# VectorE's order in the halves of an expert ring: dots, weights and rows first, its piece of attention or normalisation last

## What is computed

```python
def block_tail(x, mix, w_out, ln_g, ln_b, w_pq, sub_keys, u_tab, v_tab):
    h = layer_norm(ALPHA * x + mix @ w_out, ln_g[0], ln_b[0])
    return layer_norm(ALPHA * h + peer_ffn(h, w_pq, sub_keys, u_tab, v_tab), ln_g[1], ln_b[1])

# in peer_ffn, for a block of 128 tokens:
    q = (xb @ w_pq).reshape(PEER_BLOCK, PEER_HEADS, 2, PEER_QDIM // 2)
    s = jnp.einsum('phcd,hckd->phck', q, sub_keys).astype(jnp.float32)
    ts, ti = lax.top_k(s, PEER_TOPK)
    ...
    fs, fpos = lax.top_k(cand.reshape(PEER_BLOCK, PEER_HEADS, -1), PEER_TOPK)
    eidx = jnp.take_along_axis(cidx.reshape(PEER_BLOCK, PEER_HEADS, -1), fpos, axis=-1)
    g = jax.nn.softmax(fs, axis=-1)
    u = u_tab[eidx]
    v = v_tab[eidx]
    a = jax.nn.gelu(jnp.einsum('pd,phkd->phk', xb, u).astype(jnp.float32), approximate=False)
    return jnp.einsum('phk,phkd->pd', (g * a).astype(v.dtype), v)
```

## Time and profile before

| | us |
|---|---|
| median of 3 runs | 2391.7 |
| lowest and highest run | 2376.59, 2399.35 |
| the profiled execution | 2383.09 |
| its span (first to last instruction) | 2381.2 |

### The profile page before, as it was taken

The page is one execution under the profiler, slowest core; times in us unless marked ns, Lnnn a source line. Parts: engine busy times, 40 slices in busy tenths (PEclk is TensorE's granted clock), DMA queues, the critical chain, the costliest instruction groups (busy, mean ns, idle before and its releaser), DMA issues.

```text
span 2381.2 us, 20283 instructions
## 1 busy us (share of the span) xinstructions
PE 1797.0 (75%) x6550; PEld 1062.8 (45%) x6550; DVE 1589.9 (67%) x3264; ACT 463.7 (19%) x1078; POOL 1259.7 (53%) x1129
## 2 busy tenths in 40 slices
PE   7999772988855888758696889869968676376554
PEld 4433451966752434323364657547743334122210
DVE  2330571042297889968768998898778787667876
ACT  1110110022113425211111121111115142010110
POOL 0000000000007777876777787887777777666775
PEclk9999775556987989879798989979989898698677
DMA  3111506030219999999999999999999999999997
GB/s 130 71 71 57 38 5 235 19 142 0 89 71 357 381 382 380 339 390 395 398 395 407 410 351 380 396 376 385 411 408 399 411 409 407 414 385 407 366 372 288
DMA packets 201433, 698.14 MB, mean 293 GB/s; under 512 B 37680, under 2 KB 49648, under 8 KB 192816
## 3 DMA queue, kind: packets, MB, share of 16 engines
q0 software_dynamic: 161504, 604.58, 65.4%
q1 hardware_dynamic: 39824, 92.27, 11.4%
HBM read 690.38 MB, written 10.55 MB: 294 GB/s over the span
## 4 chain that ended last, share of the span: by engine, by line
POOL 35%; PE 16%; DVE 13%; issue 11%; DMA 11%; SPq 1%; ACT 1%; POOLq 0%; DVEq 0%; ACTq 0%
POOL arena L774 18%; POOL arena L786 17%; PE bank L807 13%; DMA arena<-in_uv,arena 8%; DVE arena L2025 3%; PE bank L2116 2%; DVE arena L2043 1%; DVE arena L1775 1%; PE bank L819 1%; POOL arena L753 1%; DVE arena L1772 1%; DMA arena<-in_w2pad 1%; DMA arena<-in_w_pq 1%; DMA arena<-in_kwin 1%; DVE arena L1777 1%
## 5 line engine op out<-in xcount | busy, mean ns | idle before, releaser
L807 PE MATMUL bank<-arena 128*128 128x512 f32 (+14 forms) x4740 | 1366.6, 449 | 476.9 <-DMA arena<-in_uv,arena 292.7
L807 PEld LDWEIGHTS bank<-arena 128*128 128x128 f32 (+4 forms) x4740 | 804.9, 203 | 995.7 <-issue 698.6
L774 POOL DMA_INDIRECT arena<-in_uv,arena x544 | 611.3, 1124 | 530.4 <-DVE arena L1833 333.8
L2025 DVE CUSTOM_DVE_ANT_0 arena<-arena 128x1024 f32<-128x1024 f32 x544 | 649.5, 1226 | 230.9 <-DMA arena<-in_uv,arena 224.0
L786 POOL DMA_INDIRECT arena<-in_uv,arena x544 | 612.7, 1126 | 185.6 <-issue 157.9
L2043 DVE SCALAR_TENSOR_TENSOR arena<-arena 128x1024 f32<-128x1024 f32 x274 | 352.1, 1285 | 37.8 <-DMA arena<-in_uv,arena 28.5
L2116 PE MATMUL bank<-arena 128*128 128x512 f32 (+13 forms) x972 | 314.6, 484 | 44.5 <-DMA arena<-in_w_in 14.3
L1631 ACT ACTIVATE arena<-arena 128x128 f32<-128x128 f32 (+1 forms) x265 | 90.9, 389 | 850.2 <-DVE arena L2035 850.1
L2116 PEld LDWEIGHTS bank<-arena 128*128 128x128 f32 (+3 forms) x972 | 159.7, 199 | 198.8 <-issue 161.1
L739 POOL DMA_DIRECT2D arena<-out_p_kc x2 | 1.4, 686 | 376.7 <-DMA out_p_vc<-arena 376.7
L819 PE MATMUL bank<-arena 128*128 128x128 f32 (+3 forms) x732 | 120.8, 305 | 45.8 <-ACT arena L1334 17.4
(11 more groups left out here) (234 smaller groups left out, 771.6 us busy)
## 6 DMA issues: line engine op xcount, KB each, us to landing
arena<-in_w_pq SPq DMA_DIRECT2D x10, 2048.0 KB, 10.4
arena<-in_uv,arena POOLq DMA_INDIRECT x1088, 8.3
arena<-in_w_in SPq DMA_DIRECT2D x6, 2048.0 KB, 7.8
arena<-in_w_out SPq DMA_DIRECT2D x6, 2048.0 KB, 12.0
arena<-in_w SPq DMA_DIRECT2D x4, 2048.0 KB, 12.9
arena<-in_w_pq SPq DMA_DIRECT2D x8, 1024.0 KB, 18.5
arena<-in_subk SPq DMA_DIRECT2D x3, 1024.0 KB, 8.9
arena<-in_xT SPq DMA_DIRECT2D x1, 2176.0 KB, 8.5
```

Of the source, the lines that this page charges most:

```text
L774: nc.gpsimd.indirect_dma_start(uv[buf(h, r)][:, 0:D], None, half_rows, bass.IndirectOffsetOnAxis(eidx_u[:, t, s0 + r:s0 + r + 1], 0))\
L807: return te.matmul(out, l, r, start=start, stop=stop)
L2025: last = ve.tensor_tensor_reduce(out=uv[b][:, 0:D], in0=uv[b][:, 0:D], in1=x_sb[:, t, :], scale=1.0, scalar=0.0, op0=ALU.mult, op1=ALU.add ...
```

## The change

In VectorE's loop the pieces of half h move from the head of the half to behind its weights and rows, ahead of its retrievals. ScalarE takes the `std` of an output normalisation before its pieces, and `NORMS` follows VectorE's new order. GpSimd's, SyncE's and TensorE's programs are the same.

```diff
@@ NORMS @@
         for h in range(N_HP):
-            NORMS += [("in", t) for t, k in ((2, K_LN[2]), (3, K_LN[3]), (PT, K_NORM)) if AFTER[k] == h]
             if h in H0[1:]:
                 NORMS.append(("out", H0.index(h) - 1))
+            NORMS += [("in", t) for t, k in ((2, K_LN[2]), (3, K_LN[3]), (PT, K_NORM)) if AFTER[k] == h]
@@ ScalarE @@
                 sc.activation(gel[:, h4], dots[:, h4], ACT.Gelu).then_inc(s_gl, 1)
+                if h in H0[1:]:
+                    std("out", H0.index(h) - 1, P)
                 for _ in range(pieces_at(h)):
                     next(todo)
-                if h in H0[1:]:
-                    std("out", H0.index(h) - 1, P)
                 half_diagonals(h)
@@ VectorE @@
             for h in range(N_HALL):
-                for _ in range(pieces_at(h)):
-                    next(todo)
                 if h + 1 < N_HALL:
                     dot_rows(h + 1)
                 if h in H0[1:]:
...
                     layer_norm("out", t, PB).then_inc(s_fin, 1)
                     settle(s_fin)
                 weigh_rows(h)
+                for _ in range(pieces_at(h)):
+                    next(todo)
                 for _ in retrievals_at(h):
                     next(late)
```

## The result

The changed kernel takes 2393.45 us (median of 20 runs, 2383.97 to 2400.12). The kernel before, run beside it, takes 2386.14 us (20 runs, 2376.59 to 2399.35). The ratio is 1.0027, with a 95% interval of 1.0014 to 1.0040: about 6 us slower, which is inside the 1% called no change. The profiled execution took 2395.28 us, its span 2393.5.

The account below looks back on a forecast made before the run. GpSimd's issue rate was taken to bound the expert stage, with a 417 GB/s DMA ceiling where weights also load. Terms +2 - 4 + 5.3 - 4 + 2 = +1.3 us on the 2391.7 median gave 2393; range 2366 to 2420.

Parts of the forecast that it names:

- Half 87, +5.3 forecast, bounds +1 and +9: Start of sample attention: TensorE's products come 10 us later for VectorE's moved copy, less 4.7 us of dots waits: net +5.3 us.
- I take 1783, between them and nearer to the late end: Half 87: assumed time of VectorE's moved copy, now at 1769.63; latest 1785.2, earliest 6.7 us before that.
- The early end: Half 87: copy 6.7 us before 1785.2, if the dots start where the piece stood and their rows have landed.
- The next step: Half 87: from copy to TensorE's first products, 0.3 us of copy plus 1.75 us taken, so products at 1785.
- These 62 us are all that any order of VectorE can win here: Expert stage: GpSimd's waits, 34.7 us for dots, 25.9 for TensorE's rows, 1.7 for VectorE's rows, bound any gain.
- Normalisations, -4 and -4 forecast: Input normalisations at halves 33 and 35, and 112: dots come first, GpSimd's 5.42 and 6.65 us waits shrink; -4 us each.
- Attention, +2 forecast: Halves 0 to 27: exps and diagonals wait for later maxima, 3.4 us left at half 19; +2 us, bounds 0 and 38.
- The slower rival: Attention halves: maxima, exps, diagonals and rows in one line outgrow the cover at low clock; +38 us, 2430; chance 0.16.
- GpSimd's price, +2 forecast: GpSimd issues that no longer wait run beside VectorE's weighing, one slower by 1.0 us at two places; +2, bounds 0 and 3.
- Other issues unchanged: Profile forecast: beyond the waits at halves 36, 115 (gone) and 89 (4 to about 14 us), GpSimd's issues stay the same.
- The ceiling: Expert stage already full of DMA transfers: gains don't come, half 87 and dearer issues still cost; 2401 us, chance 0.14.
- Nothing but gains: Half 87's copy early enough or its delay hidden, waits for dots vanish; 2375 us, 2357 with all 34.7; chance 0.14.

## Why the prediction was right, and where it was not

The time given was 2393, the time measured 2393.45, and no change was the forecast. But that is two errors which cancel. The base was the median of three runs, 2391.7; over 20 runs it is 2386.1, 5.6 lower. And the sum was +1.3 us where about +6 (3 to 10) was measured. From the better base the same sum would have said 2387. The sign held, and so did the mechanism at half 87, but the wait behind its copy was sized too small, and a cost in halves 70 to 86 stood nowhere in the sum.

**Half 87, +5.3 forecast, bounds +1 and +9; 8 to 13 by the runs, +5.5 in the changed kernel's stretch.** The mechanism is shown: the wait sits where it was said, appears with half 87 alone and goes with the copy. Its size was set by the step "I take 1783, between them and nearer to the late end". Measured against the first v issue of half 89 (1787.57 before, 1795.16 after), the copy moved from 17.94 us ahead of it to 2.32 ahead, 15.6 later: to 0.1 us the late end, 1785.2 - 1769.63. The early end supposed that the dots might move up into the piece's place. They could not: VectorE stood 3.83 us for the rows' landing before them. The next step, 0.3 + 1.75 us from the copy's start to the end of the products, measured 3.04, after TensorE had idled 9.44 us. The first block's four transposes then took 1.11 us, where the kernel before has

```profile
1774.97 0.66 PE L819 MATMUL bank<-arena 128*128 128x128 f32 x4
```

The window 1795:1815 of the changed kernel (columns as in the earlier trace rows):

```profile
1795.00:1815.00 20.00, 14.53 (x33) 5.11 (x32) 9.04 (x18) 4.55 (x9) 3.60 (x3) 0.50 0.93 366
```

and the same work in the kernel before:

```profile
1775.00:1795.00 20.00, 12.81 (x34) 4.53 (x34) 13.26 (x27) 4.55 (x9) 10.66 (x11) 0.74 1.03 405
```

A granted clock of 0.50 is 1.2 GHz throughout; 0.74 is a mixture of both levels. Against that issue the products were 13.3 us late, not 10 (2.2 from the copy, 1.0 from the products), and the wait grew by 13.0. Less the 4.7 us of the waits for dots, which went as said, that is +8.4 by GpSimd's queue, within the bounds and near the upper one. In the two runs with half 87 late and its neighbours not, a wait for dots of 1.75 and 2.91 us stayed; there the same balance is 18.81 + 1.75 - 8.66 = 11.9 and 17.99 + 2.91 - 8.66 = 12.2 us (8.66 being the three waits of the earlier trace rows). The runs' 8, 10.5 and 13 us lie around these.

In the changed kernel the stretch from 86 to 92 nevertheless grew by only 5.5 us, since GpSimd's issues in it took 3.5 us less (57.4 to 53.9 us busy). So the +5.3 is met there by luck: the wait was 3 us longer than forecast, and the cheaper issues were not forecast. This stretch is steady over the fourteen profiles:

| order in halves 87 to 91 | profiles | us from 86 to 92 |
|---|---|---|
| old | 7 | 79.6 to 80.4 |
| half 87 late, its neighbours not | 2 | 90.7, 92.0 |
| all late (the changed kernel; all but the normalisations) | 2 | 85.9, 86.1 |
| all late but the copy | 3 | 76.5 to 78.4 |

So the copy costs some 9 us beside late neighbours, 11 beside early ones, and the late neighbours give 3 to 5 of them back. With half 87 alone late, VectorE's piece of half 88 waits for TensorE ahead of the dots of half 89; in the changed kernel these dots come first. VectorE in the timeline of half 87 alone:

```profile
1804.20 0.69 DVE L1933 COPY arena<-bank 128x512 f32<-128x512 f32 x1 [16.27 <-PE bank L809]
```

**Halves 70 to 86, nothing forecast; +3.0 in the pair of profiles.** The stretch is 194.0 to 195.7 us in the four profiles with the new order there and 189.0 to 191.3 in the ten others, without overlap; the means are 4.7 apart. GpSimd hardly waits there in any of them (2 us at most). Its issues were dearer: 152.4 to 154.0 us busy against 147.2 to 149.6. "These 62 us are all that any order of VectorE can win here" left this out: not only GpSimd's waits changed with the order, but also the time of its issues. The price for dearer issues was looked for at two places only, where issues no longer wait. The runs agree in sign (copy early and all else late 0.9983, normalisations alone 0.9969), but none has these halves alone, and what makes the issues dearer is not shown; a run with the new order in halves 70 to 85 alone would price it.

**Normalisations, -4 and -4 forecast; -6.4 to -7.9 together.** Right as a sum: 7.4 and 7.9 us in the two runs that take them without half 87, 6.4 in the changed kernel. Half 112 alone gave 3.3. Halves 33 and 35 alone gave no time, though their wait went and their stretch became shorter. Together they seem to give more than apart (0.31% against 0.14 + 0.02), but the half-widths make 0.23%, so this stays open. The stretch from 109 to 119 is 134.8 to 137.1 us in the five profiles with half 112 late and the tail's pieces behind half 109 early, 139.1 to 142.5 in the five with both early, 137.2 to 140.0 in the three with both late, and 135.9 in the one with these pieces late and half 112 early. So in the changed kernel the gain of half 112 comes at best in part: the other late pieces of the tail shorten the same stretch, and the two don't add. With one profile on one side that is a reading, not shown.

**Attention, +2 forecast; 0 (within 4 us).** The cover was read rightly. In the changed kernel no v issue of halves 2 to 29 waits over 0.7 us; at half 19 TensorE's rows came free 15.65 us after the weights' multiply (14.5 worked out). I chose near the lower end and could have chosen it. The slower rival is out, by this run and by the profile, although the granted clock in 715:1025 was 0.82, a little below the 0.85 before.

**GpSimd's price, +2 forecast: not shown as a total.** The mean of a u issue went from 1124 to 1106 ns, of a v issue from 1126 to 1127, together 9.2 us less. But the total of all u and v issues is anywhere from about 1210 to 1230 us over the fourteen profiles, and about 1210 with half 87 or half 112 alone late, so 9 us are within the scatter. Of the issues over 1.85 us, 105 before and 89 after, only 10 and 5 stood behind a wait for dots; the step looked only at issues that such waits concern. Dearer in every profile with the new order were the issues of halves 70 to 86.

**"Other issues unchanged"** was wrong: in the tail, halves 110 to 117, waits for dots turned into waits for TensorE's rows (27.8 us of both kinds before, without those of 0.3 us; 31.9 after, and 2.9 for VectorE's own rows). In halves 44 to 50 they did so too (8.7 us for dots before, 11.9 for rows after), but two of the three other profiles with the new order there kept 10.0 us of waits for dots, so the order alone doesn't decide it. In the tail the sum of such waits doesn't tell the time: it is 29.1 us with the normalisations alone, which is 7.4 us faster than the kernel before.

**The rivals.** The ceiling is out: with nothing but the normalisations' gains the kernel is 0.31% faster, and 2100:2160 rose to 414 GB/s. The rule of the Trainium skill ("SBUF — State Buffer", section "A bandwidth-pool intuition that's wrong (but worth ruling out)"), about 358 GB/s to a core, is again exceeded here, at 409 and 414 GB/s over 60 us; by it the normalisations' gain could not have come. "Nothing but gains" is out with half 87; most waits for dots did go (34.7 to 8.7), but many came back at TensorE's rows.

**The sum, measured.** By the runs: half 87 +8 to +13, normalisations -6.4 to -7.9: about +3, against +6 (3 to 10) for the whole. By the stretches, as means of the profiles with the changed kernel's order there less those with the old one: halves 28 to 37 -4.5, 70 to 86 +4.7, 86 to 92 +5.9, 109 to 119 -2.2, together +3.9 (half 109 left aside); in the other stretches the two groups overlap. Both sums lie within the interval, so the +6 is accounted for only to some 3 us. The best kernels of the series leave half 87 and the attention alone: 2379.3 and 2379.9 us.

## What to carry to other kernels

When a block of work is moved back in an in-order queue, list for every iteration which other engine needs that block's output in the same iteration: one copy of 0.29 us, needed by TensorE at once, cost more than three normalisations gave. Put a moved instruction at the end of what it is moved behind, unless the trace shows that this can start earlier; where it waits for landings, it can't. And move only the iterations that gain: the rest gave nothing that a run showed, and a loss can hide among them where no engine waits, in issues that take longer (halves 70 to 86).

## What the runs showed of the hardware that was not expected

The same code differs from execution to execution by stage, not evenly: the stretch from the first u issue to that of half 28 took 311.4 us in the profile of before and 312.4 to 320.4 in those of kernels that have the same order there. The changed kernel's 318.0 looks like +6.6 us of attention, and the run with the attention late shows none of it, within 4 us. The stretch from 86 to 92, in the seven profiles with the old order there, stayed within 0.8 us. A stretch of one profile says where a wait is; what it costs needs runs, or the same stretch in many profiles.
